# Two transformer blocks on one core: the input's norm moved beside mv, late constants awaited where read, root tables loaded ahead, wo squared in PSUM

## What is computed

```
h = rms_norm(x, g_pre_mix); proj = h @ w_in            # attention, indexer, retention, memory and gate columns
mem_kv = rms_norm(mem, g_mem) @ w_mem_kv               # memory keys and values
mixed = gate_a * (o_a @ w_a) + gate_b * (o_b @ w_b) + gate_c * (o_c @ w_c)
x = x + rms_norm(mixed @ w_out, g_post_mix)            # "wo"
x = x + rms_norm((silu(f_gate) * f_up) @ w_ffn_out, g_post_ffn)   # "fo0", "fo1"
# second block, modulated: rmsnorm(x, g) * (1 + scale) + shift, with shift, scale, gate = silu(c) @ mod_w + mod_b
x = x + gate * s5_mixer(...)                           # state-space mixer, "so" is its last product
x = x + gate * nsa_mixer(...)                          # compressed, selected and window attention
out = rmsnorm(x, final_norm_g)
```

## Time and profile before

| | |
|---|---|
| median of three runs | 3204.12 us |
| profiled execution, its own time | 3198.25 us |
| its span (first to last instruction) | 3196.2 us |
| PE busy, share of the span | 97% |
| DVE busy | 69% |
| ACT busy | 47% |
| mean granted TensorE clock | 0.991 of 2.4 GHz |
| moved from HBM | 683 MB, 214 GB/s |

### The profile page before, as it was taken

How to read it: one execution, slowest core, us unless ns; L and a number is a source line. 1 busy time by engine, 2 the same in 40 slices (tenths; PEclk the granted TensorE clock), 3 DMA queues, 4 the chain that set the end, 5 groups by cost and what they waited for, 6 DMA issues and landing times.

```text
span 3196.2 us, 55870 instructions
## 1 busy us (share of the span) xinstructions
PE 3107.5 (97%) x20884; PEld 2791.9 (87%) x20884; DVE 2194.7 (69%) x2939; ACT 1504.9 (47%) x2057; POOL 119.7 (4%) x147
## 2 busy tenths in 40 slices
PE   6999999999999998999999999799999899999998
PEld 6899899888888888999889998699898899888887
DVE  5767777657767756878446665999855547566665
ACT  5455444454443455334433344656544433455553
POOL 0000000000000000000000000344100000000000
PEclk9999999999999999999999999899999999999999
DMA  5766676557777865878557775344455468644445
GB/s 210 252 236 219 234 273 212 171 171 279 274 254 273 284 234 191 320 277 318 188 193 265 258 256 185 110 144 149 137 184 171 155 236 298 221 154 152 152 145 184
DMA packets 191468, 688.79 MB, mean 216 GB/s; under 512 B 21904, under 2 KB 26256, under 8 KB 189968
## 3 DMA queue, kind: packets, MB, share of 16 engines
q1 hardware_dynamic: 183744, 669.07, 60.7%
q10 hardware_dynamic: 7504, 16.56, 1.5%
HBM read 683.45 MB, written 2.10 MB: 214 GB/s over the span
## 4 chain that ended last, share of the span: by engine, by line
PE 83%; DVE 11%; ACT 3%; DMA 2%; issue 1%; ACTq 0%; DVEq 0%; SPq 0%
PE psum L701 43%; PE psum L684 33%; DVE ring_parts L2038 3%; DVE work L2216 2%; DMA ring<-in_stream 1%; PE psum L784 1%; DVE arena_high L2221 1%; PE psum L728 1%; DVE arena_high L2222 1%; ACT hi_parts L1210 1%; PE psum L895 1%; DVE work L2178 1%; DVE work L2179 1%; PE psum L715 1%; DVE early L2166 0%
## 5 line engine op out<-in xcount | busy, mean ns | idle before, releaser
L2038 DVE TENSOR_TENSOR ring_parts<-ring,hi_parts 128x1024 fp32r<-128x1024 f32 x1002 | 1191.6, 1222 | 454.4 <-ACT hi_parts L1210 447.9
L1210 ACT ACTIVATE hi_parts<-ring 128x1024 fp32r<-128x1024 f32 x1002 | 1026.7, 1057 | 682.7 <-DMA ring<-in_stream 670.0
L684 PE MATMUL psum<-arena_low_parts,hi_parts 128*128 128x256 f32 x6048 | 1121.8, 286 | 12.4 <-DVE arena_low_parts L1782 8.9
L684 PEld LDWEIGHTS psum<-arena_low_parts,hi_parts 128*128 128x128 f32 x6048 | 951.4, 192 | 31.5 <-issue 13.1
L684 PE MATMUL psum<-arena_low_parts,ring_parts 128*128 128x256 f32 x3088 | 875.4, 283 | 0.0
L701 PE MATMUL psum<-hi_parts,arena_high_parts 128*128 128x512 f32 x2224 | 730.3, 394 | 0.0
L701 PE MATMUL psum<-hi_parts,arena_low_parts 128*128 128x512 f32 x2064 | 672.3, 392 | 2.8 <-DVE ring_parts L2038 2.6
L684 PEld LDWEIGHTS psum<-arena_low_parts,ring_parts 128*128 128x128 f32 x3088 | 594.3, 192 | 0.0
L701 PEld LDWEIGHTS psum<-hi_parts,arena_high_parts 128*128 128x128 f32 x2224 | 417.9, 188 | 89.3 <-issue 2.6
L701 PEld LDWEIGHTS psum<-hi_parts,arena_low_parts 128*128 128x128 f32 x2064 | 388.3, 188 | 84.6 <-DVE ring_parts L2038 3.9
L701 PE MATMUL psum<-ring_parts,arena_low_parts 128*128 128x512 f32 x1184 | 461.4, 390 | 0.0
(11 more groups left out here) (352 smaller groups left out, 2127.7 us busy)
## 6 DMA issues: line engine op xcount, KB each, us to landing
ring<-in_stream SPq DMA_DIRECT2D x1272, 512.0 KB, 4.2
arena_high<-in_mem ACTq DMA_DIRECT2D x2, 1024.0 KB, 5.8
arena_high<-in_x ACTq DMA_DIRECT2D x1, 2048.0 KB, 12.2
arena_low<-in_x ACTq DMA_DIRECT2D x1, 2048.0 KB, 9.7
arena_high<-in_ssm_bc ACTq DMA_DIRECT2D x64, 32.0 KB, 2.4
arena_high<-in_ssm_bc ACTq DMA_DIRECT2D x16, 128.0 KB, 3.2
out<-arena_low SPq DMA_DIRECT2D x4, 512.0 KB, 3.4
arena_high<-in_decay ACTq DMA_DIRECT2D x1, 1024.0 KB, 4.9
```

Source lines behind the costliest of these rows:

```text
L684: mm = pe.matmul(bank[:, half:half + S], r32(w[:, slot, cols]), r32(x[part][:, k, :]), start=(k == 0 and n == 0), stop=(k == KT - 1 and n ...
L1210: act.activation(r32(hi[:, g % RING, cols]), ring[:, g % RING, cols], ACT.Copy).then_inc(hi_made, 1)
L2038: dve.tensor_tensor(r32(slot), slot, as32(hi[:, g % RING, cols]), ALU.subtract).then_inc(cut_done, 1)
```

## The change

The steps, one by one:

1. `mv` leaves the first entry of `MOD_RUNS`: the 32 mod units of pieces 0 and 1 stand beside 65 units (mq to ak) instead of 73. Their sums lie where the input x lies until it is turned.
2. In `mixer_steps` the input's norm is moved: its squares, root and scaling ("rms", "x") come behind unit 0 of mk instead of ahead of it, the rope's angles behind unit 4, and the eight turns ("norm", "x", j) stand beside mv, between the five parts of the state-space parameters, instead of beside mk.
3. `late_landed` is awaited in the steps that read the constants (PE: `cmp_hidden`; DVE: the first kvt evacuations), not ahead of NSA.
4. `load_root_table` takes a root of a one into an unused column of `stat`, so that the table of the root is loaded there: before the memory's squares, at the head of `branch_and_sum` (wo and fo1), and at unit 15 of so and no.
5. wo's chunks are squared by ACT straight from PSUM (`wo_square`), and DVE's product with the gain row reads PSUM too and frees the bank; the copies go. For the last chunk, wo's and fo1's, DVE makes the sum and mean of the squares first and the product with the gain row behind them.

```
-MOD_RUNS = [(("mv", "mq", "ik", "iq", "rq", "rk", "rv", "aq", "ak"), (0, 1)), ...
+MOD_RUNS = [(("mq", "ik", "iq", "rq", "rk", "rv", "aq", "ak"), (0, 1)), ...
-    s = [("norm", "mem", j) for j in range(KT // 2)] + [("rms", "x")]
-    s += spread("mk", [("norm", "x", j) for j in range(KT // 2)] + [("angles",)])
-    s += spread("mv", [("s5_params", part) for part in range(5)]) + spread("mq")
+    s = [("norm", "mem", j) for j in range(KT // 2)] + spread("mk", [("rms", "x"), ("angles",)])
+    x_norm = [("norm", "x", j) for j in range(KT // 2)]
+    params = [("s5_params", part) for part in range(5)]
+    s += spread("mv", x_norm[:2] + params[:1] + x_norm[2:4] + params[1:2] + x_norm[4:6] + params[2:3] + x_norm[6:] + params[3:])
+    s += spread("mq")
...
+                    pe.wait_ge(late_landed, 16)          # PE, cmp_hidden, behind free_side
-            pe.wait_ge(late_landed, 16)                  # PE, ahead of steps(NSA)
+                    dve.wait_ge(late_landed, 16)         # DVE, units 1, 3, 5, 7 of kvt
-            dve.wait_ge(late_landed, 16)                 # DVE, ahead of steps(NSA)
...
+            def load_root_table():
+                did(act.activation(stat[:, 44:45], ones[:, 0:1], ACT.Sqrt))
+                did.wait()
             def branch_and_sum(n, tag, square_tile):
+                load_root_table()
...
-            def copied_square(c, t):
-                copy_bank("wo", 2 * c + t, y[:, t, c * CHUNK:(c + 1) * CHUNK])
-                act.wait_ge(*emptied(B0["wo"] + 2 * c + t))
-                square("wo", c, t)
+            def wo_square(c, t):
+                b = B0["wo"] + 2 * c + t
+                if c or t:
+                    act.wait_ge(res_squares, TT * c + t)
+                act.activation(work[:, TMP[0], :], stream_bank(b), ACT.Square,
+                               accum_out=stat[:, 32 + 4 * t + c:33 + 4 * t + c]).then_inc(res_squares, 1)
...
                 elif phase in ("so", "no") and u and (u % 4 == 0 or u == 15):
+                    if u == 15:
+                        load_root_table()
                     squares_of_sum("x3" if phase == "so" else "out", (u - 1) // 4)
...
+            act.wait_ge(consts_made, CONSTS_MADE)
+            load_root_table()
             squares("mem", mem_in, tokens(0)[:, 0, :], mem_landed)
...
                 dve.wait_ge(res_squares, TT * (4 * n + c) + t + 1)
-                did(dve.tensor_tensor(y[:, t, cols], y[:, t, cols], row[:, cols], ALU.mult))
+                if n == 0:
+                    b = B0["wo"] + 2 * c + t
+                    dve.tensor_tensor(y[:, t, cols], stream_bank(b), row[:, cols], ALU.mult).then_inc(evacuated[b % 4], 1)
+                else:
+                    did(dve.tensor_tensor(y[:, t, cols], y[:, t, cols], row[:, cols], ALU.mult))
...
             def add_branch(n, t):
-                times_gain(n, 3, t)
-                did.wait()
+                dve.wait_ge(res_squares, TT * (4 * n + 3) + t + 1)
                 then(dve.tensor_reduce(stat[:, 40 + t:41 + t], stat[:, 32 + 4 * t:36 + 4 * t], AX, ALU.add))
                 dve.tensor_scalar(stat[:, 40 + t:41 + t], stat[:, 40 + t:41 + t], 1.0 / D, EPS, ALU.mult,
                                   ALU.add).then_inc(res_mean, 1)
+                times_gain(n, 3, t)
+                if n == 0:
+                    dve.wait_ge(*emptied(B0["wo"] + 6 + t))
```

More of the change, by code:

```diff
@@ L59 @@
 PIECES = ["s5_scale", "s5_shift", "s5_gate", "kv_shift", "kv_scale", "nsa_shift", "nsa_scale", "nsa_gate"]
-MOD_RUNS = [(("mv", "mq", "ik", "iq", "rq", "rk", "rv", "aq", "ak"), (0, 1)), (("mix",), (3, 4)), (("ff0",), (5, 6)), (("ff1",), (2,)),
+MOD_RUNS = [(("mq", "ik", "iq", "rq", "rk", "rv", "aq", "ak"), (0, 1)), (("mix",), (3, 4)), (("ff0",), (5, 6)), (("ff1",), (2,)),
             (("kvn", "nq"), (7,))]
@@ L1219, in square @@
                                accum_out=stat[:, at:at + 1]).then_inc(res_squares, 1)
[L1221 to L1225 removed]
+            def wo_square(c, t):
[4 more added lines that the diff above has]
+                               accum_out=stat[:, 32 + 4 * t + c:33 + 4 * t + c]).then_inc(res_squares, 1)
             def last_of_wo(t):
                 act.wait_ge(*((first_tile_done, ENDS["wo"]) if t == 0 else multiplied("wo", 15)))
[L1230 removed]
+                wo_square(3, t)
             def last_of_fo1(t):
@@ L1274, in unit @@
                     for t in range(TT):
-                        copied_square(c, t)
+                        wo_square(c, t)
                 elif phase == "mix" and u % MIX_HALF + 1 in MIX_GATES:
@@ L2007, in unit @@
                 elif phase == "wo" and u % 4 == 3 and u < 15:
+                    dve.wait_ge(*multiplied(phase, u))
                     for t in range(TT):
@@ L2141, in _ @@
             for t in range(TT):
+                dve.wait_ge(*((first_tile_done, ENDS["wo"]) if t == 0 else multiplied("wo", 15)))
                 add_branch(0, t)
```

1 line of the change is left out of this document (removed).

## The result

The changed kernel took **3177.82 us**, median of six runs (3175.90 to 3183.57); the kernel before took 3203.39 in the six runs beside it. The ratio is 0.9928, with a 95% interval of 0.9917 to 0.9938, which is 19.9 to 26.6 us less. A second comparison, of five further runs against sixteen, gave 0.9936 (0.9923 to 0.9950), 16 to 25 us less. The profiled execution took 3179.62 us (span 3177.8), 18.6 less than before's. One run of the later kernel a_table took 3844.82 us at a granted clock of 0.75, a slower state of the chip that no other run showed, and is left out.

The account below looks back on a forecast made before the run. PE, busy 97% of the span, bounds the kernel; its waits and half clock were the targets. Terms -0.9 - 7.2 - 1.5 - 2.0 - 0.5 - 0.5 - 4.2 = -16.8 us, so 3204.1 becomes 3187 us, range 3180 to 3196.

Parts of the forecast that it names:

- The start, -0.9: At the start, the root table loaded before the memory lands lets its root begin at about 10.5 instead of 11.4 us.
- The norm, -7.2 and -1.5: In mk, the 8.56 us wait shrinks by 7.2 us to short new waits; the half clock behind it goes, 1.5 us.
- The turns beside mv, nothing: In mv, eight moved turns of 0.44 us cost nothing, DVE's part hidden by PE; up to 7 us without that cover.
- The rival of 7 us: In mv, DVE's small steps and turns delay cuts or turns, costing up to 7 us: 3194 us, chance 0.12.
- Denser modulation units, -2.0: From mq to ak, density costs 1.8 us, while rv's wait and clock dip go, -3.8 us; together -2.0 us.
- seven places: In iq, rq, rk, rv, aq and ak, only one unit between two modulation units; priced at 1.8 us in all.
- The other half, the wait of 2.1 us: At rv, the needed cut comes some 2.3 us earlier, so the wait (2.1) and half-clock dip (1.7) go: -3.8 us.
- wo, -0.5: Behind wo, no copy and the mean before the gain product, limited by ACT's square of the sum: -0.5 us.
- fo1, -0.5: Behind fo1, table ahead and mean before gain take 0.5 us off the 7.48 us wait.
- so, -4.2: Behind so, earlier scaling gives 0.9 us and no wait for the late constants 3.3 us; the shift passes on whole.
- My split: Behind so, 0.9 us for the table loaded ahead and 3.3 us for the later await of the constants.
- signs that would have shown it wrong: mq starting after 122 us, new cut-unit waits from mq to ak above 6 us, or x3's turns waiting for something else.

Follow-up runs that it names:

- a_table: The changed kernel without the three root tables loaded ahead; median 3179.44 us of three runs.
- before_again: The kernel before, unchanged, profiled and run once more; median 3200.85 us of ten runs.
- b_mods: The kernel before with only the modulation units moved, beside 65 units instead of 73; median 3198.71 us, ratio 0.9988.
- a_late: The changed kernel with PE and DVE awaiting the late constants ahead of the NSA steps again; median 3182.14 us.
- a_dense: The changed kernel with the 32 modulation units beside 48 units (rq to ak) instead of 65; median 3188.25 us.

## Why the prediction was right, and where it was short

The direction and the places were right; the size was 16.8 us for 20.5 to 23.1. The forecast of 3187.0 lies 9 us above the first median and 6 above the second, and the range's low end of 3180 lies between the two.

**The start, -0.9:** 14.85 to 13.94. a_table gives it back.

**The norm, -7.2 and -1.5:** 9.3 us against before_again, of which 1.1 is edit 1's in mv; the norm's own 8.2 is 0.5 less than forecast. The new wait was 0.74 us and not 1.2, and the 0.2 ahead of unit 1 was 0.27 at 26.6 us. My estimate of the cut's time was late by half a microsecond. The half clock was right in size for the profile that I read, where PE worked for 3.1 us at the half level; behind the same wait it was 2.8 us in before_again and 6.0 in b_mods.

**The turns beside mv, nothing:** mv took 47.34 us, the 43.8 of products and 3.5 of turns that I had added up, and there is no wait in the chain. The 43.8 held two short waits that went with the modulation units: mv is 43.54 us without them (b_mods), so the turns made it 3.8 longer. The rival of 7 us did not come.

**Denser modulation units, -2.0:** this step failed in its size. I counted seven places with only one unit between two modulation units and priced them at 1.8 us; they cost nothing (b_mods, PE busy 87.20 of 87.20). The count of places was the wrong measure, and so is DVE's fill, which was 24.61 of 26 us in rv with PE never idle. I also missed the 1.1 us in mv. The other half, the wait of 2.1 us, went as said. The 1.7 us of half clock behind it I took as sure; it comes in some executions only.

**wo, -0.5:** -0.9, with the tables giving nothing. **fo1, -0.5:** the wait fell by 0.28, and as it was 7.20 us without the table too (a_table), that is the mean ahead of the gain; but the stage gained nothing, as DVE came 0.3 us later to the small step ahead of it (1.58 us of wait instead of 1.31).

**so, -4.2:** -5.0 to -6.0. My split was wrong (0.9 for the table, 3.3 for the constants): with the constants awaited the table gives nothing (a_late), without them it gives 0.2 (a_table). And I had said that the turns pass the shift on whole; they also became faster, 2.53 us instead of 3.68 for 16 matmuls, as the clock fell only at 2471.42 us, 1.2 us into the turns, where in the kernel before it had fallen 3.1 us ahead of them, at 2485.11. PE had stood for 3.6 us and not for 8.

In sums of the table's stages, with a fast unit 0 on both sides and with the half clock at rv: 0.9 + 9.3 + 3.7 + 0.9 + 0 + 5.0 = 19.8 us. The 3.0 us above the forecast are 1.7 at rv, 0.8 at so, 0.6 in mk and mv together and 0.4 at wo, less 0.5 at fo1. Errors of both signs are in this: the density that cost nothing and the 1.1 us in mv that I had not counted made the gain larger, the norm's move (0.5) and fo1 (0.5) smaller. To that extent the total is nearer than its terms by luck. The ratios of the runs say 20.5 and 23.1 us. The 1 to 3 us beyond the stages are not settled. Part may be unit 0, which had the half level in two of five profiles with the late start and in three of nine with the early one; so few do not show it, and stages like ff0 wander by more.

Of the signs that would have shown it wrong none came: mq began at 115.6 us (limit 122, forecast 118.5, of which 2.1 is the faster unit 0), PE had no wait on a cut unit between mq and ak, and the turns of x3 waited for DVE's scaling, 3.60 us for the 4 forecast. Those behind wo and fo1 waited 8.29 and 7.20 us for 8.7 and 6.9.

## What to carry to other kernels

Whether added work on an engine with idle time is free was told here neither by its mean over a stage, nor by its fullest 26 us, nor by a count of crowded places. Look at the order ahead of the instruction that is waited for, how long the engine takes from one such instruction to the next, against the time of the waiting engine; and push the density until it breaks, which gives the limit. Where two things are awaited at one point, remove the later one first: the table was worth nothing as long as the constants came later. With runs that scatter by 10 us, parts of 1 us are to be read in stages that repeat, and a stage that wanders in a second profile of the same kernel is no evidence.

## What was not expected of the hardware

The moment at which the clock first rises differs between executions of the same program: 12 or 23 matmuls in the 2.4 us from 20.0, in before and before_again. Unit 0 was slow in five of 14 profiles, the clock rose at 22.7 to 24.1 us in these and at 16.9 to 19.1 in the others, and it cost 1.7 to 2.1 us. The views print a granted clock of 1.00 for the time ahead of the first record, so the level must be read there from the spacing of the products.

The fall of the clock behind a wait of 2.1 us came in two profiles of three, and behind the wait of 8.56 us PE worked at the half level for 2.8 to 6.0 us in four profiles of the same order. Behind the waits of up to 1.80 us in the changed kernel's ff0 there was no fall. Behind one of 1.87 us in a_dense there was (timeline of PE, then the stretch behind it), and behind an equal one at 2064.3 us of that profile there was none:

```profile
2216.39 1.08 PE L1068 MATMUL psum<-arena_high 128*32 128x128 f32 x32 [1.87 <-DVE arena_high L2245]
```

```profile
2217.60:2220.90 3.30, 3.30 (x39) 2.61 (x39) 3.30 (x5) 0.00 (x0) 0.80 (x2) 0.50 0.08 26
```

A short wait on a cut unit cost about 0.3 us more than its idle time (1.1 us for two waits of 0.50 in all).
